# A ninth 2 MB load buffer in rotation, loop bodies of three pairs, and the down biases moved to the last pair but one

## The reference

```
logits = h @ w_router + b_router ; top-4, softmax over the chosen -> combine (256 x 32)
for e in range(32):
    gu   = h @ w_gu[e] + b_gu[e]                     # 1024 -> 2048
    gate = min(gu[:, :1024], 7) ; lin = clip(gu[:, 1024:], -7, 7)
    act  = gate * sigmoid(1.702 * gate) * (lin + 1)
    out += combine[:, e:e+1] * (act @ w_down[e] + b_down[e])
return rmsnorm(x + out, g_final)
```

## Time and profile before

| | |
|---|---|
| median of 3 runs | 1038.89 us (1037.91 to 1041.66) |
| the profiled execution's own time | 1037.48 us |
| its span in the profile | 1034.8 us |
| PE busy | 956.8 us (92%) |
| DVE, ACT, POOL busy | 284.8, 133.7, 18.2 us |
| moved by DMA | 419.41 MB, 405 GB/s over the span |
| chain that ended last | PE 53%, DMA 41%, DVE 4% |

### The profile page before, as it was taken

The page is one execution under the profiler, slowest core; times in us unless marked ns, Lnnn a source line. Parts: engine busy times, 40 slices in busy tenths (PEclk is TensorE's granted clock), DMA queues, the critical chain, the costliest instruction groups (busy, mean ns, idle before and its releaser), DMA issues.

```text
span 1034.8 us, 12029 instructions
## 1 busy us (share of the span) xinstructions
PE 956.8 (92%) x4841; PEld 427.4 (41%) x4841; DVE 284.8 (28%) x537; ACT 133.7 (13%) x200; POOL 18.2 (2%) x20
## 2 busy tenths in 40 slices
PE   7999999999999989989899999989898999989895
PEld 7988443434343333434243243434343343424331
DVE  6954331222221213122121213113121312213113
ACT  7634001010100000000000000000000000000102
POOL 0500000000000000000000000000000000000000
PEclk9999999999999999999999999999999999999999
DMA  9569899999999999999999999999999999999993
GB/s 359 205 261 396 343 380 415 428 428 430 429 426 429 429 429 428 430 429 426 429 429 429 428 430 429 426 429 429 428 428 430 429 426 429 429 428 428 428 427 146
DMA packets 34489, 419.41 MB, mean 405 GB/s; under 512 B 5300, under 2 KB 5960, under 8 KB 9864
## 3 DMA queue, kind: packets, MB, share of 16 engines
q1 hardware_dynamic: 34432, 419.16, 96.1%
q10 hardware_dynamic: 40, 0.01, 0.0%
HBM read 418.10 MB, written 1.05 MB: 405 GB/s over the span
## 4 chain that ended last, share of the span: by engine, by line
PE 53%; DMA 41%; DVE 4%; issue 1%; ACT 0%; SPq 0%; ACTq 0%; DVEq 0%
PE ps L909 50%; DMA raw<-in_w_down 37%; DMA raw<-in_w_gu 3%; PE ps L1142 2%; DVE woutl L653 1%; DVE xT L750 1%; DMA win<-in_w_in 1%; PE ps L1193 0%; ACT sm L477 0%; PE ps L998 0%; DVE mxs L670 0%; DVE sm L665 0%; PE ps L1166 0%; DVE outs L900 0%; PE ps L1052 0%
## 5 line engine op out<-in xcount | busy, mean ns | idle before, releaser
L909 PE MATMUL ps<-raw,xT 128*64 128x512 f32 x2048 | 459.6, 597 | 23.1 <-DMA raw<-in_w_gu 22.8
L909 PEld LDWEIGHTS ps<-raw,xT 128*64 128x64 f32 x2048 | 140.9, 137 | 322.0 <-issue 265.1
L909 PE MATMUL ps<-raw,actT 128*64 128x512 f32 x1024 | 233.4, 597 | 24.6 <-DMA raw<-in_w_down 24.6
L909 PEld LDWEIGHTS ps<-raw,actT 128*64 128x64 f32 x1024 | 72.2, 136 | 161.2 <-issue 147.4
L840 DVE TENSOR_TENSOR biased<-ps,biasT 128x1024 f32<-128x1024 f32 x32 | 39.2, 1224 | 335.5 <-PE ps L1142 335.5
L541 ACT ACTIVATE gu<-ps 128x1024 f32<-128x1024 f32 x32 | 32.8, 1024 | 527.8 <-PE ps L909 527.8
L857 DVE TENSOR_TENSOR acc<-ps,acc 128x512 f32<-128x512 f32 x64 | 41.2, 686 | 135.4 <-PE ps L909 135.4
L750 DVE TENSOR_TENSOR xT<-ps,gT 128x512 f32<-128x512 f32 x32 | 22.1, 691 | 180.1 <-PE ps L909 180.1
L909 PE MATMUL ps<-ysc,dispT 64*128 64x512 f32 x272 | 67.8, 615 | 0.8 <-DVE ysc L891 0.8
L909 PEld LDWEIGHTS ps<-disp,h 128*128 128x128 f32 x512 | 61.6, 196 | 12.4 <-issue 12.2
L909 PE MATMUL ps<-disp,h 128*128 128x128 f32 x512 | 64.8, 285 | 0.2 <-DVE disp L744 0.2
(11 more groups left out here) (163 smaller groups left out, 428.6 us busy)
## 6 DMA issues: line engine op xcount, KB each, us to landing
raw<-in_w_gu SPq DMA_DIRECT2D x128, 2048.0 KB, 32.6
raw<-in_w_down SPq DMA_DIRECT2D x64, 2048.0 KB, 34.7
win<-in_w_in SPq DMA_DIRECT2D x16, 512.0 KB, 12.5
wout<-in_w_out SPq DMA_DIRECT2D x4, 1024.0 KB, 9.4
acc<-in_x SPq DMA_DIRECT2D x2, 512.0 KB, 3.8
out<-outs SPq DMA_DIRECT2D x2, 512.0 KB, 3.1
gfin<-in_g_final SPq DMA_DIRECT2D x1, 512.0 KB, 9.5
cst<-in_consts SPq DMA_DIRECT2D x1, 402.0 KB, 7.7
```

The source lines that it names most:

```text
L909: return pe.matmul(out_, lhsT, rhs, start=start, stop=stop, skip_group_check=shared)
```

## The change

- `RAW` is 9. The ninth buffer lies at 128 to 144 KB per partition, where `xT` and `gu` lay; these go to 168 and 172 KB. Unit n is issued once unit n - 9 is used. Unit 8 is issued by hand after `logits`, at the place where `gfin` was loaded.
- 12 units times three pairs is four turns of nine buffers, so the body holds three pairs: one pair (the first) stands ahead of the loop, three behind it, and the loop runs four times. The number of further rounds is counted in threes of pairs.
- The first pair has no scatter. The down biases go into `bdown` (182 KB, the place of `comb2`) and the turned `comb2` into `combT`; both are multiplied in the scatter of iteration 14 (`biases=True`), two more matmuls in each of two calls.
- POOL no longer zeroes `ysc` and `dispT`; it zeroes rows 32 to 127 of `bgu`, and `bdown` once `comb_turned` is raised. SP loads `b_down` behind that.
- The transposes of the gate/up biases become matmuls over 128 rows against the identity.
- `gfin` is loaded at the end, behind the last unit; `outs` and `gfin` lie in a buffer of the ring that is free by then.
- On DVE the copy of the expert numbers `i8` to float (`i4`) goes; the comparison reads `i8`.

```diff
-RAW = 8
-PLACE = (2, 3, 6, 7, 0, 1, 4, 5)
+RAW = 9
+PLACE = (2, 3, 6, 7, 0, 1, 4, 5, 8)
...
+ROUND_TRIPLES = (6, 5, 5, 0)
+MORE = sum(ROUND_TRIPLES)
...
-        xT = at("xT", [P, DC, 2, SLOTS], F32, 136 * KB)
-        gu = at("gu", [P, FE], F32, 140 * KB)
+        xT = at("xT", [P, DC, 2, SLOTS], F32, 168 * KB)
+        gu = at("gu", [P, FE], F32, 172 * KB)
...
+        bdown = at("bdown", [P, 512], F32, 182 * KB)
+        combT = at("combT", [P, TT, P], F32, 195 * KB + 256)
...
-        gfin = at("gfin", [P, D], F32, 128 * KB)
-        outs = at("outs", [P, TT, D], F32, 168 * KB)
+        gfin = at("gfin", [P, D], F32, 112 * KB)
+        outs = at("outs", [P, TT, D], F32, 116 * KB)
...
@@ SP
             load(1, 1, 5)
-            sp.wait_ge(ysc_zeroed, 1)
-            for h in range(2):
-                sp.dma_start(ysc[h * SLOTS:h * SLOTS + E, 0, :], b_down[0, :, h * 512:(h + 1) * 512]).then_inc(bdown_loaded, 16)
             sp.wait_ge(half_projected, 1)
             load(1, 2, 6)
             sp.wait_ge(projected, 3)
             load(1, 3, 7)
-            sp.dma_start(bgu[:], b_gu[0]).then_inc(bgu_loaded, 16)
+            sp.dma_start(bgu[0:E, :], b_gu[0]).then_inc(bgu_loaded, 16)
             sp.wait_ge(logits, 2)
-            sp.dma_start(gfin[:], g_final.rearrange("(a n) -> a n", a=1).broadcast_to([P, D])).then_inc(gfin_loaded, 16)
+            load(0, GU_U, RAW - 1)
             sp.wait_ge(rounds_ready, 1)
...
-                    sp.wait_ge(unit_used, i * ITER_U + PRE_U + at_ - RAW + 1)
+                    sp.wait_ge(unit_used, i * ITER_U + (PRE_U + at_ - RAW + 1))
...
-            with sp.Fori(0, last_two) as j:
-                iteration(j, 0, False)
-                iteration(j, 1, False)
-            iteration(last_two, 0, False)
-            iteration(last_two, 1, True)
+            sp.wait_ge(bdown_zeroed, 1)
+            for h in range(2):
+                sp.dma_start(bdown[h * SLOTS:h * SLOTS + E, :], b_down[0, :, h * 512:(h + 1) * 512]).then_inc(bdown_loaded, 16)
+
+            iteration(None, 0, False)
+            with sp.Fori(0, triples) as j:
+                for third in range(3):
+                    iteration(j, third, False)
+            iteration(triples, 0, False)
+            iteration(triples, 1, False)
+            iteration(triples, 2, True)
+            sp.wait_ge(unit_used, number(triples, 2) * ITER_U + PRE_U)
+            sp.dma_start(gfin[:], g_final.rearrange("(a n) -> a n", a=1).broadcast_to([P, D])).then_inc(gfin_loaded, 16)
...
@@ POOL
-            pool.wait_ge(attended, 2)
-            pool.memset(ysc[:, 0, :], 0.0).then_inc(ysc_zeroed, 1)
             pool.wait_ge(projected, 3)
             pool.memset(comb2[:], 0.0).then_inc(comb2_zeroed, 1)
-            pool.memset(dispT[:, 1, :, :], 0.0).then_inc(dispT_zeroed, 1)
-            pool.wait_ge(scaled, TT)
-            pool.memset(ysc[:, 1, :], 0.0).then_inc(ysc_zeroed, 1)
+            pool.wait_ge(comb2_zeroed, 1)
+            pool.memset(bgu[E:2 * E, :], 0.0).then_inc(bgu_zeroed, 1)
+            pool.wait_ge(bgu_zeroed, 1)
+            pool.memset(bgu[2 * E:P, :], 0.0).then_inc(bgu_zeroed, 1)
+            pool.wait_ge(bgu_zeroed, 2)
+            pool.wait_ge(comb_turned, 1)
+            pool.memset(bdown[:], 0.0).then_inc(bdown_zeroed, 1)
...
@@ DVE
-                link(dve.tensor_copy(i4[:, t, :], i8[:, t, 0:K]))
...
@@ PE
-            def scatter(t):
+            def scatter(t, biases):
                 for h in range(2):
                     rows = slice(h * SLOTS, (h + 1) * SLOTS)
+                    if biases:
+                        mm(ps[:, M[h], :], combT[rows, t, :], bdown[rows, :], stop=False)
...
-                    ins = pe.transpose(ps[:, 2, col * E:(col + 1) * E], src, c_("ident", E)[:, 0:E])
+                    ins = mm(ps[:, 2, col * E:(col + 1) * E], src, c_("ident")[:, 0:E], start=col == 0,
+                             stop=col == 2 * DC - 1, shared=True)
...
+            iteration(None, 0, False, first=True)
+            with pe.Fori(0, triples) as j:
+                for third in range(3):
+                    iteration(j, third, False)
+            iteration(triples, 0, False)
+            iteration(triples, 1, False, biases=True)
+            iteration(triples, 2, True)
```

More of the change, by code:

```diff
@@ L279, in pair_of, with unit, number @@
             return i % PAIRS
[L281 to L288, removed]
+        def unit(j, third, k):
+            if j is None:
+                n = PRE_U + k
+                return n % RAW, (n // RAW + 1) * 16
+            n = ITER_U + PRE_U + third * ITER_U + k
+            return n % RAW, j * (3 * ITER_U // RAW * 16) + (n // RAW + 1) * 16
+        def number(j, third):
+            return 0 if j is None else j * 3 + (third + 1)
         block = ctx.enter_context(nc.Block())
@@ L353, in iteration @@
                     at_ = k - (GU_U if last and k >= 2 * GU_U + DN_U else 0)
-                    sp.wait_ge(unit_used, i * ITER_U + PRE_U + at_ - RAW + 1)
-                    s = buffer(half, at_)
+                    sp.wait_ge(unit_used, i * ITER_U + (PRE_U + at_ - RAW + 1))
+                    s = unit(j, third, at_)[0]
                     if k < GU_U + DN_U:
@@ L538, in gu_copy @@
                 act.wait_ge(unit_used, used)
-                if not isinstance(e, int):
+                if not (isinstance(e, int) and e == 0):
                     act.wait_ge(gu_turned, e)
@@ L574, in iteration @@
                     act.activation(ysc[0:SLOTS, 1, :], ps[0:SLOTS, Y[1], :], ACT.Copy).then_inc(outputs_ready, 1)
-            with act.Fori(0, last_pair) as i:
+            iteration(0, False)
+            with act.Fori(1, last_pair) as i:
                 iteration(i, False)
@@ L884, in iteration @@
                     clip(i * 2 + 2, e)
-            with dve.Fori(0, last_pair) as i:
+            iteration(0, False)
+            with dve.Fori(1, last_pair) as i:
                 iteration(i, False)
@@ L1144, in turn_gu @@
                 ins.then_inc(gu_turned, 1)
-            def scatter(t):
+            def scatter(t, biases):
                 for h in range(2):
                     rows = slice(h * SLOTS, (h + 1) * SLOTS)
+                    if biases:
+                        mm(ps[:, M[h], :], combT[rows, t, :], bdown[rows, :], stop=False)
                     for a in range(2):
-                        ins = mm(ps[:, M[h], :], dispT[rows, a, t, :], ysc[rows, a, :], start=a == 0, stop=a == 1)
+                        ins = mm(ps[:, M[h], :], dispT[rows, a, t, :], ysc[rows, a, :],
+                                 start=a == 0 and not biases, stop=a == 1)
                     ins.then_inc(scattered, 1)
@@ L1165, in _, with iteration @@
                     src = bgu[:, h * FE:(h + 1) * FE].rearrange("e (u q r) -> e u r q", q=P, r=4)[:, m // 4, m % 4, :]
-                    ins = pe.transpose(ps[:, 2, col * E:(col + 1) * E], src, c_("ident", E)[:, 0:E])
+                    ins = mm(ps[:, 2, col * E:(col + 1) * E], src, c_("ident")[:, 0:E], start=col == 0,
+                             stop=col == 2 * DC - 1, shared=True)
             ins.then_inc(bias_turned, 1)
-            pe.wait_ge(bdown_loaded, 32)
-            pe.wait_ge(ysc_zeroed, 2)
-            pe.wait_ge(dispT_zeroed, 1)
             turn_gu(0)
             pe.wait_ge(biasT_ready, 1)
-            last_two = pe.snap(pe.value_load(further[0:1, 0:1], min_val=0, max_val=T // SLOTS - 1) * (PAIRS // 2) + (PAIRS // 2 - 1))
-            def iteration(j, half, last):
-                i = j * 2 + half
+            triples = pe.snap(pe.value_load(further[0:1, 0:1], min_val=0, max_val=MORE) + 4)
+            def iteration(j, third, last, first=False, biases=False):
+                i = number(j, third)
                 for k in range(DC):
-                    gu_unit(1, k, *unit(j, half, k // 2))
+                    gu_unit(1, k, *unit(j, third, k // 2))
                     if k == 1:
-                        pe.wait_ge(outputs_ready, i * 2 + 1)
                         pe.wait_ge(gate_clipped, i * 2 + 1)
                         pe.wait_ge(up_clipped, i * 2 + 1)
-                        scatter(0)
-                    if k == 2:
-                        pe.wait_ge(added, i * 4 + TT + 2)
-                        scatter(1)
+                    if k == 1 and not first:
+                        pe.wait_ge(outputs_ready, i * 2)
+                        if biases:
+                            pe.wait_ge(bdown_loaded, 32)
+                            pe.wait_ge(combT_ready, 1)
+                        scatter(0, biases)
+                    if k == 2 and not first:
+                        pe.wait_ge(added, i * 4 - 4 + (TT + 2))
+                        scatter(1, biases)
                     if k == 3:
-                        pe.wait_ge(added, i * 4 + TT + 3)
+                        if not first:
+                            pe.wait_ge(added, i * 4 - 4 + (TT + 3))
                         pe.wait_ge(gated_ready, i + 1)
```

(9 more changed lines are left out.)

72 lines of the change are left out of this document (36 added, 36 removed).

## The result

| | before | changed |
|---|---|---|
| median of 8 runs each | 1038.98 us (1036.9 to 1041.66) | 1042.0 us (1040.9 to 1043.48) |
| ratio, 95% interval | | 1.0037 [1.0021, 1.0053] |
| the profiled execution's own time | 1037.48 us | 1043.4 us |
| its span | 1034.8 us | 1041.6 us |

The changed kernel is slower by 3.8 us by the ratio (2.2 to 5.5) and by 3.0 by the medians, under the half per cent taken as telling. Forecast: +3.3 us and 1042.2.

What follows compares the result with a forecast made beforehand. The prediction took the weight stream, at 428 GB/s, to bound the kernel. Its terms, 11.8 - 4.9 - 3.6 and 0, summed to +3.3 us: 1042.2 us, own range 1039.5 to 1044.5, overall 1036 to 1046.

Steps and rivals of the forecast that it cites:

- The bound: Whole kernel from 380 us on: the weight stream at 428 GB/s sets 58.7 us a pair; PE needs 53.6.
- Term 3: Stream's restart: SP's wait for bdown_zeroed holds unit 9 until about 120.6 us, where unit 8 left at 108.78; +11.8 us.
- The removed CAST: On DVE before the restart: could bring it forward by 0 to 0.43 us; taken as 0.
- Term 1: Hole at 104 to 109 us: unit 8 issued early at 99.72 leaves 183 units, not 184, after the restart; -4.9 us.
- Term 2: Stream at 112 to 176 us: buffers from unit 13 on free some 15 us early, so holes go; -3.6 us.
- Term 4: Everything else, bias matmuls (+2.1 us on PE at most), loop of three and late gfin: covered, 0 us.
- the stream's lead over PE at unit 16: First unit of iteration 1: stream has it at 162 us, PE needs it at 173.8; lead some 11 us.
- Rival A: At the restart: loads are not held, unit 9 leaves at 108.78 + 0.80; sum -7.7, time 1031.2 us; chance 0.08.
- B: Rival, 112 us to the end: stream slower per unit; 1% is 9.0 us, time 1051.2 us; chance 0.08.
- C: Rival at the end: gfin lands 1.3 us after DVE's need; +1.3 us, time 1043.5 us; chance 0.08.
- the turn to the stream's pace at about 290 us: Sign in the chain: pairs turn from PE's 53.6 us to the stream's 58.7 at about 290 us, not 380.
- SP's wait on POOL: Sign in SP's list of waits: its wait on POOL's memset of bdown stands at the top.

Runs made afterwards that it cites:

- e1: Changed kernel with SP's wait for bdown_zeroed and the two b_down loads moved behind the first pair's loads; 1036.39 us, ratio 0.9969 to the kernel before.
- e2: Kernel before, with one wait added: SP waits for comb_turned ahead of its loop; 1044.7 us, ratio 1.0053 to the kernel before.
- e3: Changed kernel with unit 8 issued behind the two b_down loads instead of after the router's logits; 1045.76 us, ratio 1.0065 to the kernel before.
- e10: As e4, but unit 8 issued after the read of the number of rounds, as in the kernel before; 1034.87 us, ratio 0.9956 to the kernel before.
- e6: Changed kernel, wait left in, only the gate/up bias matmuls put back to 32-row transposes; 1042.38 us, ratio 1.0029 to the kernel before.
- e4: As e1, with the gate/up bias transposes of the kernel before (32 rows, no zeroing of bgu); 1031.34 us, ratio 0.9924 to the kernel before.
- e8: e4 once more, on another chip beside e5 to e7; 1030.93 us, ratio 0.9925 to the kernel before.
- e5: As e4, plus unused dummy matmuls on PE (4.0 us) where the first pair had two scatter calls; 1036.07 us, ratio 0.9972 to the kernel before.
- e7: As e4, plus 14 identity matmuls on PE at the start, while it waits for w_in; 1031.37 us, ratio 0.9919 to the kernel before.

## Why the prediction was right

**The bound.** Right. 58.73 against 58.72 us a pair, and a plateau of 428 GB/s in both kernels.

**Term 3, +11.8.** Right. Unit 9 left at 123.20 - 2.5 = 120.7; forecast 120.6. That is +11.9 on 108.78. Its links held too: POOL began 0.12 us after PE's transposes (I had 0.03), the memset took 0.53, the two loads 0.79. The removed CAST brought nothing: the six `mask` matmuls start at 104.36 - 2.5 = 101.9, before at 101.76. e1 and e2, which take the hold out of one kernel and put it into the other, show that it decides the sign. In e3, where nothing has to be taken off, the `b_down` loads leave at 119.84 and the next unit at 120.66.

**Term 1, -4.9.** Right within what can be told: 4.9 between the traces of e3 and the changed kernel, 2.9 to 3.8 in the times of e3 and 3.3 to 3.9 in those of e10, with intervals that reach 4.9.

**Term 2, -3.6.** Right. From 124 to 176 us the changed kernel loses 52 x (1 - 422/428) = 0.7 us, but all of it before 126 us, where the stream is only starting again, since unit 9 left at 123.20:

```profile
124.00:126.00 2.00, 2.00 (x10) 2.00 (x10) 0.00 (x0) 0.00 (x0) 0.00 (x0) 0.77 0.99 246
126.00:176.00 50.00, 49.22 (x242) 22.28 (x241) 11.26 (x23) 3.91 (x5) 0.00 (x0) 0.94 1.01 429
```

From 126 us on it has no hole. The kernel before has 396 GB/s in the second of these stretches. With this the sum is 11.9 - 4.9 - 3.6 = +3.4, and the traces, once aligned, differ by +4.3. No row explains the 0.9 between them; half of it could be the 429 and 428 GB/s from 176 to 400 us, which is one step in the last digit.

**Term 4, 0.** The result was right; a price in it and the reason for it were wrong. The bias matmuls cost 5.5 us more on PE, more than the upper bound of 2.1. I had doubled the old time for more rows; but the 16 transposes are 16 records with weights of 32 rows, and the 16 float32 matmuls are 32 records with weights of 128 rows. That the 5.5 us cost nothing is shown by e6. My reason was the stream's lead over PE at unit 16, but work added to PE only makes that lead larger. What must not run out is the margin of the buffers, which term 2 put at 15 us. SP's issues of units 10 to 13:

```profile
123.67 11.67 SPq L330 DMA_DIRECT2D raw<-in_w_gu  x4
```

Unit 13, the last of them, leaves at 135.0. The stream restarts at about 125 us, and units 9 to 12 last it for 4 x 4.9 us, to about 144.6 (an estimate from these rows). The margin is 9.6 us, the 15 less the 5.5. In e1, where the stream isn't held, there is no such margin, and the same 5.5 us cost 4.7.

**Rival A** was priced at 1031.2 for the wait alone. e1 has 1036.4: with the hold gone, the bias matmuls came onto the path, which I had not looked for behind it. With these undone too, e4 and e8 have 1031.3 and 1030.9. Of B and C there is no sign: the rate is the same, and neither POOL nor DVE waits for `gfin`.

**What missed:** the turn to the stream's pace at about 290 us. In the chain it came at 326.9 - 2.5 = 324 (before: 380), and PE's first wait for a unit after the early stages, which is where the lead is used up, at 342.85 - 2.5 = 340 (before: 381.6). PE comes to unit 16 at 180.75 - 2.5 = 178.3 and not at 173.8, so the lead was some 16 us and not 11; at 5.1 us a pair that is three pairs, which fits 340. The bias matmuls, which my 173.8 leaves out, are enough for it. SP's wait on POOL was the third of its list and not the top.

**What was luck.** The forecast of 1042.2 is 0.2 us from the median, closer than the working deserves. The eight runs fall into two groups, four from 1040.9 to 1041.2 and four from 1042.8 to 1043.5, and the median lies in the gap between them. The ratio leaves +2.2 to +5.5. And term 4 was priced at less than half of what it was; it did no harm because the hold of term 3 covered it.

## What to carry to other kernels

Where a stream of transfers is at its limit, do its accounts: when does it stand still, and how many bytes are left when it starts again. The time a buffer gains is lost when a small load with a wait of its own stands ahead of the stream in the same in-order queue; put such a load behind the next big ones, and its wait costs nothing that can be seen here (e4). And when a long stall is taken away, price again everything that it covered: behind the hold the bias matmuls were worth nothing (e6) and the scatters made no hole (e2, 430 GB/s from 124 us), and without it they were worth 4.7 and 4.9 us (e1 against e4, e5).

## What the runs showed of the hardware

**Slower runs mostly have a lower granted clock.** The twelve runs of e1 go from 1033.8 to 1038.8 us, and each has its mean granted clock beside it:

```
mean clock 0.994: 1033.8 1033.9 1033.9 1034.1
mean clock 0.992: 1035.2 1035.7
mean clock 0.990: 1037.1 1037.2 1037.6
mean clock 0.988: 1038.4 1038.7 1038.8
```

0.006 of 1035 us is 6.2 us of full clock not granted, and the time rises by 4.8. The slowest run of e4, of e5, of e6, of e8 and of e10 has the lowest clock of its kernel too. It is no strict rule: the kernel before, beside e1, has 1037.48 and 1041.23 us at the same 0.995. From 176 to 1000 us the clock is 1.00 in every trace, so what is lost is lost outside of that. The reading that fits e1's trace is that it matters up to unit 4 of the first pair, where PE releases the stream (0.76 from 124 to 140 us); the other eleven runs have no trace, so this is argued and not shown.

**Where it falls.** The start of the changed kernel's profiled run shows one such place (stretches 8 to 12 and 12 to 16 us):

```profile
8.00:12.00 4.00, 0.20 (x2) 0.00 (x0) 2.07 (x4) 2.33 (x4) 0.00 (x0) 1.00 1.00 401
12.00:16.00 4.00, 3.87 (x20) 3.90 (x21) 4.00 (x8) 3.95 (x8) 0.00 (x0) 0.57 1.04 423
```

and in the kernel before:

```profile
8.00:12.00 4.00, 1.27 (x11) 1.06 (x10) 3.27 (x6) 3.48 (x7) 0.00 (x0) 1.00 1.03 419
12.00:16.00 4.00, 4.00 (x36) 4.00 (x35) 4.00 (x7) 3.83 (x6) 0.00 (x0) 1.00 1.02 409
```

The first piece of `w_in` landed 1.1 us later. PE was idle for 3.9 us instead of 2.7, started its projection at 12.13 us instead of 10.98, and had 0.57 of its clock in the next stretch, that is 1.2 GHz for most of these 4 us: 20 matmuls where the other run did 36. By the first expert the 1.1 us have become the 2.5 by which the trace is shifted. e6's profiled run shows it again: PE starts its projection at 12.07 us, the clock is 0.50 from 12 to 16 us, and the first expert begins at 109.92. In e7's, where PE had work in the wait, the delay did not grow. The Trainium skill (TensorE: Matmul & The Clock Gate, Part 1) says that the moment at which the clock changes differs from run to run of the same kernel; the same program here had both, e4 with clock 1.00 in 112 to 176 us and e8 with 0.97.

**The clock also fell while PE was busy.** In the changed kernel PE was on the bias matmuls from 121.52 us, without a gap, and the clock fell under them, to 0.77 in the stretch 124 to 126 us and to 0.50 in the next:

```profile
126.00:128.00 2.00, 2.00 (x11) 2.00 (x10) 0.00 (x0) 0.00 (x0) 0.00 (x0) 0.50 0.98 418
```

**A small matmul with many rows is not small.** 32 records of 128x32 with 128x128 weights took 7.57 us, 237 ns each, of which part at half clock; the transposes that they replace took 131 ns each and there were 16.

**Open.** Why e5's twelve runs are 4.9 us longer where its trace has 3.1 to 3.4 us more of idle stream; whether the bridge of e7 removes the slower runs; and where in e1's slower runs the clock was lost, since only one of the twelve has a trace.
